# The last residual add of an encoder trunk: from two VectorE passes to two TensorE products and one VectorE pass

## The reference, cut to what matters

```python
# grouped_moe: every token has two experts, with weights g (they sum to 1)
return jnp.zeros((T, D)).at[tok_sorted].add(ys[dest] * g_sorted[:, None])
# layer, then the end of the program
x = x + g2 * grouped_moe(...)
return rms_norm(x, norm_f)      # x * rsqrt(mean(x*x) + eps) * norm_f
```

## Time and profile before

| what | value |
|---|---|
| median of 3 runs | 1601.59 us (1600.87 to 1603.16) |
| profiled execution, its own time | 1596.52 us |
| its span in the trace | 1595.0 us |
| TensorE (PE) busy | 1461.2 us, 92% of the span |
| VectorE (DVE) busy | 558.9 us, 35% |
| ScalarE (ACT) busy | 438.7 us, 28% |
| mean granted TensorE clock | 0.962 of full speed |

### The profile page before, as it was taken

The page is one execution under the profiler, slowest core; times in us unless marked ns, Lnnn a source line. Parts: engine busy times, 40 slices in busy tenths (PEclk is TensorE's granted clock), DMA queues, the critical chain, the costliest instruction groups (busy, mean ns, idle before and its releaser), DMA issues.

```text
span 1595.0 us, 20969 instructions
## 1 busy us (share of the span) xinstructions
PE 1461.2 (92%) x7500; PEld 805.3 (50%) x7501; DVE 558.9 (35%) x1286; ACT 438.7 (28%) x1021; POOL 86.7 (5%) x96
## 2 busy tenths in 40 slices
PE   4999999999999699999779899999999949999991
PEld 1664555777745333444236555667775523334440
DVE  0056555465732311111134464454442240111114
ACT  2326565200022111121041565541100311111211
POOL 0000002000000101100000000110000000111000
PEclk8999999999998799999979999999999969999996
DMA  9626070215260799999862433401305039999984
GB/s 359 226 85 225 14 262 4 67 54 158 63 240 40 303 417 423 419 421 425 334 243 106 155 115 113 153 1 40 106 1 211 40 142 418 422 420 422 423 369 178
DMA packets 95082, 343.55 MB, mean 215 GB/s; under 512 B 13796, under 2 KB 37956, under 8 KB 80632
## 3 DMA queue, kind: packets, MB, share of 16 engines
q1 hardware_dynamic: 69152, 305.68, 48.9%
q0 software_dynamic: 9168, 28.00, 4.7%
q10 hardware_dynamic: 16648, 8.40, 1.8%
HBM read 327.34 MB, written 17.86 MB: 216 GB/s over the span
## 4 chain that ended last, share of the span: by engine, by line
PE 84%; DMA 6%; DVE 4%; issue 2%; ACT 2%; DVEq 1%; SPq 0%; ACTq 0%; POOLq 0%
PE bank L1885 18%; PE bank L1643 11%; PE bank L1593 10%; PE bank L1896 10%; PE bank L1798 7%; PE bank L1685 6%; PE bank L1700 4%; PE bank L1710 4%; PE bank L1720 4%; DMA ring<-in_w 3%; PE bank L1626 2%; PE bank L1545 2%; PE bank L1564 2%; DMA ring<-in_w_ada 1%; PE bank L1851 1%
## 5 line engine op out<-in xcount | busy, mean ns | idle before, releaser
L1885 PE MATMUL bank<-ring,reg_b 128*32 128x512 f32 (+2 forms) x1376 | 284.1, 607 | 3.7 <-ACT reg_b L1025 3.7
L1885 PEld LDWEIGHTS bank<-ring,reg_b 128*32 128x32 f32 (+2 forms) x1376 | 95.4, 129 | 140.8 <-issue 140.8
L1593 PE MATMUL bank<-ring,hT 128*128 128x512 f32 (+3 forms) x512 | 159.3, 473 | 3.1 <-ACT hT L873 3.1
L1593 PEld LDWEIGHTS bank<-ring,hT 128*128 128x128 f32 x512 | 98.1, 193 | 59.6 <-issue 29.4
L1685 PE MATMUL bank<-reg_a,ring 128*128 128x512 f32 x256 | 112.7, 593 | 0.9 <-DVE reg_a L1234 0.9
L1025 ACT ACTIVATE reg_b<-bank,cur 128x128 f32<-128x128 f32 x176 | 63.7, 467 | 179.9 <-PE bank L1851 179.9
L1896 PE MATMUL bank<-ring,reg_b 128*32 128x512 f32 (+2 forms) x544 | 113.2, 594 | 0.0
L1798 PE MATMUL bank<-ring,reg_b 128*128 128x512 f32 x256 | 112.2, 594 | 0.0
L952 ACT ACTIVATE reg_f<-bank,nmax 128x512 f32<-128x512 f32 x128 | 87.0, 683 | 60.8 <-DVE nmax L1229 59.9
L1229 DVE TENSOR_REDUCE nmax<-bank 128x1 f32<-128x512 f32 x128 | 83.6, 685 | 48.8 <-PE bank L1700 48.5
L1643 PE MATMUL bank<-hT,ring 128*128 128x256 f32 x384 | 88.2, 380 | 0.2 <-DVE reg_f L1275 0.2
(11 more groups left out here) (258 smaller groups left out, 1780.8 us busy)
## 6 DMA issues: line engine op xcount, KB each, us to landing
ring<-in_w SPq DMA_DIRECT2D x74, 2048.0 KB, 23.7
ring<-in_w_ada SPq DMA_DIRECT2D x19, 2048.0 KB, 8.1
reg_a<-in_w SPq DMA_DIRECT2D x12, 2048.0 KB, 21.7
ring<-in_w_in SPq DMA_DIRECT2D x10, 2048.0 KB, 19.2
hT<-in_w SPq DMA_DIRECT2D x10, 2048.0 KB, 28.4
vb<-in_w_ada ACTq DMA_DIRECT2D x16, 512.0 KB, 3.9
ring<-in_w_o SPq DMA_DIRECT2D x4, 2048.0 KB, 9.2
ring<-in_w_proj_a SPq DMA_DIRECT2D x8, 512.0 KB, 11.2
```

Source lines behind the costliest of these rows:

```text
L1593: ins = pe.matmul(bank[2 + k % 4][:, 0:n], hT[:, c, t * P:(t + 1) * P], w[:, c, :], start=c == 0, stop=c == NC - 1)
L1885: ins = pe.matmul(bank[bk][at:at + n, :], xsT[:, p % 2, c, at:at + n], slot(MOE_SLOT[j, m], NC, F)[:, c, :], start=c == 0, stop=c == NC - 1)
```

## The change

VectorE first writes four diagonal matrices, diag(w1) of each tile, into `hT` (four products of the identity with `gw[:, 1, t]`). TensorE gets 16 matmuls: for each tile t and each half h of 512 columns, identity times x, then diag(w1) times y1, accumulated in `bank[2t+h]`. VectorE then forms x = w0*y0 + bank in two instructions of 512 columns each in place of two of 1024 with a drain between. It waits for each half (`xy_r`). Tile order, ScalarE's stream, the transfers and everything in the layer loop stay.

```diff
+        gw_d = hT[:, 0:4, 0:P]
...
+        gd_s = sem("weight_diagonals_ready")
+        xy_r = sem("x_and_second_output_ready")
...
+            for t in range(NT):
+                TS(gw_d[:, t, :], ident, gw[:, 1, t:t + 1], None, ALU.mult).then_inc(gd_s, 1)
             for t in range(NT + 1):
                 if t < NT:
-                    combine(DEPTH - 1, t)
+                    v.wait_ge(cg_s[t], DEPTH * 16)
+                    for h in range(2):
+                        cols = slice(h * 512, (h + 1) * 512)
+                        v.wait_ge(xy_r, 2 * t + h + 1)
+                        ins = STT(x[:, t, cols], cy[t][:, 0, cols], gw[:, 0, t:t + 1], bank[2 * t + h][:, :], ALU.mult, ALU.add)
+                    ins.then_inc(x2, 1)
                 if t:
                     u = t - 1
                     mean_square(2 * DEPTH, u)
...
+            for t in range(NT):
+                pe.wait_ge(gd_s, t + 1)
+                pe.wait_ge(cg_s[t], DEPTH * 16)
+                for h in range(2):
+                    cols = slice(h * 512, (h + 1) * 512)
+                    pe.matmul(bank[2 * t + h][:, :], ident, x[:, t, cols], start=True, stop=False)
+                    pe.matmul(bank[2 * t + h][:, :], gw_d[:, t, :], cy[t][:, 1, cols], start=False, stop=True).then_inc(xy_r, 1)
```

## The result

The changed kernel is slower. Its median is 1607.39 us (13 runs, 1602.97 to 1612.89), that of the kernel before, run beside it, 1602.82 us (13 runs). One of before's runs took 5219.71 us and is not used in the ratio; the median of its other twelve is 1602.30 us. The ratio is 1.0032 (95% interval 1.0020 to 1.0044), which is 3 to 7 us. The forecast was a gain of 1.4 us, with a range up to 1602.7 us.

What follows compares the result with a forecast made beforehand. VectorE was taken to bound the tail: -2.7 us from shorter combines of tiles 2 and 3 and +1.3 from a later tile 1 gave -1.4, so 1600.2 us, range 1598.2 to 1602.7.

Steps and rivals of the forecast that it cites:

- What bounds the kernel: Tail, behind VectorE's last expert product: VectorE sets the end, the combine is 2.55 of its 4.41 us period, TensorE idle.
- the rest of the sum's frame: Behind tile 1's combine: four pieces of 1.86 us, two combines of 2.55, then 3.05 us for the last store.
- The diagonals: Ahead of the tail's first tile: four VectorE products, 1.1 us, hidden in 9.6 us with a 3.6 us check.
- What a matmul costs: New TensorE products in the tail: 0.43 us each at full clock, 0.86 us at clock 0.50.
- the doubled price: Rival: the tail's new products run at half the rate (four passes); +2.9 us, 1604.5; chance 0.02.
- When the clock rises: TensorE's restart in the tail at about 1574.25: clock rises from 0.50 after 4.3 us, between 2.9 and 5.6.
- The first two tiles: Tiles 0 and 1 wait for TensorE; tile 1 added at 1580.7 against 1579.4, a loss of 1.3 us.
- The next two: Tiles 2 and 3: VectorE bounds again, combine 1.22 us instead of 2.55, a gain of 2.7 us, 2.4 with waits.
- a move outside the tail: Rival: something outside the tail moves by more than 3.2 us, either way; runs lie 2.3 us apart; chance 0.06.

Runs made afterwards that it cites:

- ctl_before: The kernel before, unchanged, run again against itself; ratio 0.9992 (0.9979 to 1.0005), tail 30.0 us.
- unread: The changed kernel, but its new matmuls stream constant rows, nobody reads their result and VectorE combines as before; ratio to before 1.0004, tail 29.9 us.
- after_again: The changed kernel, unchanged, run a second time; ratio to the kernel before 1.0015 (1.0001 to 1.0028), tail 32.8 us.
- warmed: The changed kernel plus eight more identity products, result overwritten, ahead of TensorE's wait for the reloaded tiles; tail 30.8 us against 33.0.
- one_product: The changed kernel without the products of the identity with x, so 8 products instead of 16; tail 29.2 us.
- ident_early: The changed kernel with the eight identity products issued ahead of the wait for the reloaded tiles; median 1600.25 us, ratio to before 0.9978, tail 27.9 us.
- halves_alone: The kernel before with one combine pass of two 512-column instructions, the second output left out, no TensorE work in the tail; tail 26.6 us.
- bf16_products: The changed kernel with both operands of the 16 products read as bfloat16, the high halves of their float32 words; tail 27.7 us.

## Why the prediction was wrong, step by step

**What bounds the kernel, and the rest of the sum's frame** held. VectorE set the end of the tail in before, and its 30.4 us became 30.0 and 29.9 where VectorE's work was left as it was (ctl_before, unread).

**The diagonals** took 0.87 us (1.1 forecast) and started 0.46 us after the last expert product; the check for extra blocks cost almost nothing here, and I had borrowed 3.6 us for it from the turn of the layers. Hidden either way.

**"What a matmul costs" is the step that failed.** I took 16 records in 7.03 us for 16 matmuls of the program. They are eight: the code at that line runs over two halves and four chunks. So 0.43 us was the price of a record and 0.86 that of a product, 1.71 at the low clock. The row was read against itself and never against the loop that issues it. The rule I set against it was right: the Trainium skill, page "FP8 and Floating Point Precision", section "TensorE Precision Notes", has four passes for true FP32, and the measured 0.86 us x 2.4 GHz / 512 columns is 4.0, so the trace agrees. I let a miscounted row outvote it, gave the doubled price a chance of 0.02 and said that all rows of this shape spoke against it.

That rival's own sum held: +2.9 us for the tail from a rise after 4.3 us, against +2.6 and +2.8 measured.

**When the clock rises**: forecast 4.3 us after the restart, measured 4.4 in after and 3.6 in after_again. The size was right, and there was luck in the exact figure, which was only the middle between 2.9 and 5.6. With products of double cost the low clock was worth 2.1 us of the tail (warmed).

**The first two tiles**: tile 1 was to be added at 1580.7, that is 16.1 us after the head's end; measured 19.4 and 19.2. With half the products it is 16.1 (one_product).

**The next two** were to gain 2.7 us since VectorE would be the bound again. In after it is not: TensorE needs 3.43 us for a tile (eight records 0.43 apart) and VectorE 3.17 where nothing holds it up (ident_early), so the end of the kernel goes by TensorE. What follows behind tile 1 took 10.6 us, not 9.9. Where VectorE is the bound (ident_early, one_product, halves_alone) it takes 10.05, a gain of 2.5. The half on PSUM with a scalar is 0.75 us, the upper of my two bounds, and not 0.69.

**The scatter.** A range of 2.3 us over three runs made me call a move outside the tail unlikely. Twelve later runs of the unchanged kernel spanned 8.1 us (1597.86 to 1605.95), and the profiled execution was a fast one. The range up to 1602.7 was too narrow for that alone: the unchanged kernel's own median beside after was 1602.82. But it does not account for the miss, since after was slower than the before that ran beside it, by a ratio of at least 1.0020.

## What to carry to other kernels

Before pricing an instruction from a group's count, divide the count by what the loops of the source issue; here one float32 product of 512 columns is two records and takes 0.86 us at full clock. When work moves to an idle engine, count that engine's time per tile against the period that it must keep up with, and issue what does not depend on the late input ahead of the wait: that was worth 5 us of tail and kept the clock up. Compare single traces by stage. When a stage differs that the edit does not touch, trace the unchanged kernel a second time before you blame the edit.

## What the runs showed of the hardware

A float32 product of 128x128 by 128x512 is two matmul records 0.43 us apart at full clock, a bfloat16 one a single record, 0.23 us from the next, even with operands read at every other 16-bit element. TensorE idle for 2.35 us, busy for 7.1 and idle for 0.85 kept its full clock until the tiles landed (ident_early); idle for 10.05 us (after), it restarted at half of it and rose 4.4 us later, in after_again 3.6. In bf16_products, where TensorE stood idle for 0.62 to 1.40 us between tiles, the granted clock was 1.00 for the third tile (1583 to 1585) and 0.50 again for the fourth (1586 to 1587). One wait for a transfer of weights in the same program varied from 1.24 to 2.60 us between two executions without any edit, another from 1.92 to 3.75.
